# A sparse layer's index selection placed between projection units and attention pieces, and a reordered differential attention

## The reference

```python
def dsa_mixer(h, w_in, w_out, cos_a, sin_a, cos_i, sin_i):      # sparse layer A
    q, k, v, qi, ki, wi = split(h @ w_in)     # 16 heads of q, 4 of k and v, 8 index heads, 1 index key, 8 weights
    q, k, qi, ki = (partial_rope(t) for t in (q, k, qi, ki))
    wi = wi * IDX_WEIGHT_SCALE
    score = sum_h relu(qi_h @ ki.T) * wi_h                       # one score per query and key
    score = where(key in a visible chunk, score, -inf)
    sel = top_k(score, 64)                                       # 64 keys for every query
    o = softmax(q @ k[sel].T * 64 ** -0.5) @ v[sel]
    return o @ w_out

def diff_attention(h, w_qkv, w_o, ...):                          # layer C, 272 tokens
    q, k, v = split(h @ w_qkv)                                   # 8 heads, two maps c = 0, 1 of 64 columns each
    p = softmax(where(key <= query, q_c @ k_c.T * 64 ** -0.5, min))
    a = p[0] - lam * p[1]
    o = rmsnorm(a @ v, subln_g) * (1 - lambda_init)              # over the 128 columns of a head
    return o @ w_o
```

## Time and profile before

| what | before |
| --- | --- |
| median of 3 runs | 1735.62 us |
| lowest and highest | 1734.61 and 1742.96 us |
| the profiled execution, its own time | 1721.73 us |
| its span (first to last instruction) | 1719.9 us |
| granted TensorE clock, mean | 0.994 |
| PE, DVE, ACT busy | 96%, 61%, 44% of the span |

### The profile page before, as it was taken

How to read it: one execution, slowest core, us unless ns; L and a number is a source line. 1 busy time by engine, 2 the same in 40 slices (tenths; PEclk the granted TensorE clock), 3 DMA queues, 4 the chain that set the end, 5 groups by cost and what they waited for, 6 DMA issues and landing times.

```text
span 1719.9 us, 30972 instructions
## 1 busy us (share of the span) xinstructions
PE 1656.5 (96%) x12658; PEld 1548.7 (90%) x12658; DVE 1051.0 (61%) x1261; ACT 757.0 (44%) x1007; POOL 6.4 (0%) x21
## 2 busy tenths in 40 slices
PE   7899999998999999999999999999999999999998
PEld 5858999987899998999987999979999796789997
DVE  7785765458666556666457665466554647576653
ACT  3345553432655434444445444444443336454442
POOL 0000000010000000000000000000000000000000
PEclk9989999999999999999999999999999999999999
DMA  7602566633146675556722556635575351235671
GB/s 168 165 25 74 171 187 180 190 101 105 44 147 194 172 196 167 173 179 185 194 76 90 179 171 190 174 101 171 172 207 158 111 182 51 67 123 180 197 205 61
DMA packets 346674, 252.99 MB, mean 147 GB/s; under 512 B 32574, under 2 KB 345820, under 8 KB 346604
## 3 DMA queue, kind: packets, MB, share of 16 engines
q1 hardware_dynamic: 345136, 250.00, 49.4%
q10 hardware_dynamic: 1468, 2.02, 0.4%
HBM read 250.95 MB, written 1.05 MB: 147 GB/s over the span
## 4 chain that ended last, share of the span: by engine, by line
PE 82%; DVE 12%; ACT 4%; DMA 1%; issue 1%; ACTq 0%; DVEq 0%; SPq 0%
PE acc L457 25%; PE acc L458 25%; PE acc L459 25%; DVE w_low L1313 2%; PE acc L610 2%; PE spare L588 1%; DVE xg_low L1357 1%; ACT w_high L915 1%; PE acc L596 1%; DVE x_state L1508 1%; DVE squares L1342 1%; PE acc L473 1%; DVE evac_a L1506 1%; ACT xg_high L920 1%; PE acc L844 0%
## 5 line engine op out<-in xcount | busy, mean ns | idle before, releaser
L1313 DVE TENSOR_TENSOR w_low<-w_raw,w_high 128x2048 fp32r<-128x2048 f32 (+3 forms) x229 | 540.6, 2361 | 415.5 <-ACT w_high L915 415.4
L457 PE MATMUL acc<-xg_high,w_high 128*128 128x272 f32 (+4 forms) x2592 | 743.9, 287 | 14.7 <-DVE w_low L1313 7.6
L915 ACT ACTIVATE w_high<-w_raw 128x2048 fp32r<-128x2048 f32 (+3 forms) x229 | 451.4, 1971 | 684.4 <-PE acc L459 645.4
L458 PE MATMUL acc<-xg_low,w_high 128*128 128x272 f32 (+4 forms) x2592 | 737.8, 285 | 0.0
L459 PE MATMUL acc<-xg_high,w_low 128*128 128x272 f32 (+4 forms) x2592 | 735.7, 284 | 0.0
L457 PEld LDWEIGHTS acc<-xg_high,w_high 128*128 128x128 f32 (+3 forms) x2592 | 485.9, 187 | 32.0 <-issue 14.4
L458 PEld LDWEIGHTS acc<-xg_low,w_high 128*128 128x128 f32 (+3 forms) x2592 | 484.7, 187 | 3.7 <-issue 3.3
L459 PEld LDWEIGHTS acc<-xg_high,w_low 128*128 128x128 f32 (+3 forms) x2592 | 484.8, 187 | 0.2
L457 PE MATMUL acc<-hidden_high,w_high 128*128 128x256 f32 (+1 forms) x1216 | 345.2, 284 | 2.2 <-DVE w_low L1313 2.1
L459 PE MATMUL acc<-hidden_high,w_low 128*128 128x256 f32 (+1 forms) x1216 | 344.5, 283 | 0.0
L458 PE MATMUL acc<-hidden_low,w_high 128*128 128x256 f32 (+1 forms) x1216 | 344.4, 283 | 0.0
(11 more groups left out here) (198 smaller groups left out, 1062.9 us busy)
## 6 DMA issues: line engine op xcount, KB each, us to landing
w_raw<-in_ffn_w_dram SPq DMA_DIRECT2D x88, 1024.0 KB, 5.3
w_raw<-in_ffn_w_dram SPq DMA_DIRECT2D x32, 1408.0 KB, 7.0
w_raw<-in_mlp_w_up_dram SPq DMA_DIRECT2D x32, 1024.0 KB, 5.4
w_raw<-in_mlp_w_down_dram SPq DMA_DIRECT2D x32, 1024.0 KB, 5.6
w_raw<-in_attn_w_qkv_dram SPq DMA_DIRECT2D x12, 1024.0 KB, 5.1
w_raw<-in_a_w_in_dram SPq DMA_DIRECT2D x18, 256.0 KB, 4.4
w_raw<-in_a_w_in_dram SPq DMA_DIRECT2D x4, 1024.0 KB, 8.1
w_raw<-in_a_w_out_dram SPq DMA_DIRECT2D x4, 1024.0 KB, 5.0
```

What stands on the lines that cost most here:

```text
L457: pe.matmul(dst, high_w, high, start=first, stop=False)
L458: pe.matmul(dst, high_w, low, start=False, stop=False)
L915: act.activation(whi[c % 2][:, 0:SIZES[c]], raw[c % 2][:, 0:SIZES[c]], ACT.Copy).then_inc(S["w_high"], 1)
L1313: dve.tensor_tensor(wlo[c % 2][:, s], raw[c % 2][:, s], whi[c % 2][:, s].bitcast(F32), ALU.subtract)\
```

## The change

In the sparse layer the chunks are reordered (index queries, index key, values with the index weights, keys, four of queries). The key unit makes its 128 columns once. Values and weights come out by tokens, as `acc[token, column]`, so their transposes go; two more small matmuls give the norm by tokens. The rope works on unscaled units that ACT copies to `plain` (part of `mixer_out`); the norm is multiplied into `cos_a` and `sin_a`. The rope turns, the eight index products (all in one bank, `spare1`) and the selection rounds are written between the k-steps of the units, the units' evacuations, and the pieces of the attention. The attention takes all pieces of block 0 and then those of block 1; the selection of block 1 and the last query rope stand beside the pieces of block 0. The 17 fillers go.

In layer C the chunks come as values, keys, queries; the value transposes stand between units; the scores of pieces 0 and 1 stand ahead of unit 11. The query scale is folded into a second norm row (`rstd2`). PE adds the causal mask by a matmul of the identity with the mask constants into the same bank; the row maximum and the exponentials read PSUM directly. `difference` combines the maps once with a ratio of the row sums, and the division comes with ACT's copy of the output. DVE copies the transposed probabilities, not ACT. Pieces go by blocks; block 0 is normalized while block 1's pieces run. The second chunk of w_o is split beside piece 4. In the third feed-forward layer's up projection 28 fp32r matmuls take the place of 7 float32 fillers.

```diff
-        Gemm("a_in", [KD * 256] * 2 + [KD * 136] + [KD * 256] * 6, 9, dmas=[1, 1, 3, 4, 4, 4, 4, 1, 1]),
+        Gemm("a_in", [KD * 256] * 2 + [KD * P] + [KD * (KV_COLS + IDX_HEADS)] + [KD * 256] * 5, 9,
+             dmas=[1, 1, 2, 2, 1, 4, 4, 4, 4]),
...
+            def turn_raw(r, tiles):
+
+                pe.wait_ge(S["rope_raw"], r + 1)
+                if r == 7:
+                    bank = acc[1][:, 1]
+                else:
+                    bank = sp[0][:, r % 2]
+                    if r >= 2:
+                        pe.wait_ge(S["rope_read"], r - 1)
+                pe.matmul(bank[:, 0:tiles * SEQ], rotA, plain[r % 4][:, 0:tiles], start=True, stop=True)\
+                    .then_inc(S["rope_turned"], 1)
+
+            def index_logits(q):
+
                 i, m = q // 4, q % 4
-                if q == 1:
-                    pe.wait_ge(S["wi_ready"], 1)
-                if q >= 2:
-                    pe.wait_ge(S["idx_relu"], q - 1)
+                if q == 0:
+                    pe.wait_ge(S["rope_done"], 3)
+                else:
+                    pe.wait_ge(S["idx_relu"], q)
                 for c in range(2):
                     r = slice(c * HD, (c + 1) * HD)
-                    ins = pe.matmul(sp[q % 2][:, c, 0:(i + 1) * P], qiA[r, m, i * P:(i + 1) * P],
+                    ins = pe.matmul(sp[1][:, c, 0:(i + 1) * P], qiA[r, m, i * P:(i + 1) * P],
                                     kiA[r, 0:(i + 1) * P], start=True, stop=True)
                 ins.then_inc(S["idx_full"], 1)
...
+            def values_by_token(j):
+
+                c, u, wide_ = g.c0 + j, g.u0 + j, KV_COLS + IDX_HEADS
+                pe.wait_ge(S["w_low"], c + 1)
+                pe.wait_ge(S["rope_raw"], 2)
+                for i in range(2):
+                    t = slice(META + i * P, META + (i + 1) * P)
+                    for k in range(KD):
+                        if i == 0 and k == 4:
+                            turn_raw(2, 1)
+                        if i == 1 and k == 6:
+                            index_logits(0)
+                        hw, lw = cols(c, k * wide_, (k + 1) * wide_)
+                        dst = acc[u % 2][:, i, 0:wide_]
+                        pe.matmul(dst, XH[:, k, t], hw, start=k == 0, stop=False)
+                        pe.matmul(dst, XH[:, k, t], lw, start=False, stop=False)
+                        ins = pe.matmul(dst, XL[:, k, t], hw, start=False, stop=k == KD - 1)
+                ins.then_inc(S["w_used"], 1)
+
+            wide(g, 0, META, SEQ, xg_waits(PAIRS))
+            sum_squares(SEQ, 1, tokens=True)
+            wide(g, 1, META, SEQ, between={4: lambda: turn_raw(0, 2)})
+            wide(g, 2, META, SEQ, tiles=key_twice, M=1, between={6: lambda: turn_raw(1, 2)}, free=(S["rope_raw"], 1))
+            values_by_token(3)
+            wide(g, 4, META, SEQ, between={0: lambda: index_logits(1), 5: lambda: index_logits(2)},
+                 free=(S["rope_raw"], 3))
+            pe.wait_ge(S["v_ready"], n.add("v_ready"))
+            wide(g, 5, META, SEQ, between={1: lambda: index_logits(3), 3: lambda: turn_raw(3, 2),
+                                           6: lambda: index_logits(4)})
+            wide(g, 6, META, SEQ, between={2: lambda: index_logits(5), 4: lambda: turn_raw(4, 2),
+                                           6: lambda: index_logits(6)}, free=(S["rope_raw"], 4))
+            wide(g, 7, META, SEQ, between={2: lambda: index_logits(7), 4: lambda: turn_raw(5, 2)},
+                 free=(S["rope_raw"], 5))
+            wide(g, 8, META, SEQ, between={4: lambda: turn_raw(6, 2)}, free=(S["rope_raw"], 6))
+            pe.wait_ge(S["rope_raw"], 7)
+            keep_busy(acc[1][:, 0], 1)
+            turn_raw(7, 2)
...
-            keep_busy(acc[0][:, 0], 17)
-            attention([(i, m) for m in range(8) for i in range(2)],
+            pe.wait_ge(S["idx_relu"], 8)
+            pe.wait_ge(S["rope_done"], 7)
+            attention([(i, m) for i in range(2) for m in range(8)],
...
+            def make_scores(p):
+
+                i, h = pieces[p]
+                nk, d0 = (i + 1) * P + META, i * P + META
+                if p >= 2:
+                    pe.wait_ge(S["exp_done"], before + p - 1)
+                for c in range(2):
+                    r = slice(c * HD, (c + 1) * HD)
+                    pe.matmul(sp[p % 2][:, c, 0:nk], qC[r, h, i * P:(i + 1) * P], kC[r, h, 0:nk], start=True, stop=False)
+                for c in range(2):
+                    ins = pe.matmul(sp[p % 2][:, c, d0:nk], ident, cst[:, C_CAUSAL + META:C_CAUSAL + META + P],
+                                    start=False, stop=True)
+                ins.then_inc(S["s_full"], 1)
...
+            for j in range(1, 11):
                 wide(g, j, 0, T2)
-            turn_v(g, 8, [(0, P), (P, P), (2 * P, META)])
+                if 4 <= j < 10:
+                    turn_values(j - 4)
+            pe.wait_ge(S["v_ready"], n.add("v_ready", 6))
+            pe.wait_ge(S["dve_evac"], g.r0 + 9)
+            make_scores(0)
+            make_scores(1)
+            wide(g, 11, 0, T2)
             begin(G["w_o"])
-            keep_busy(acc[0][:, 0], 2)
-            attention([(i, h) for h in range(DIFF_HEADS) for i in range(2)],
-                      lambda i, h: [(qC[c * HD:(c + 1) * HD, h, i * P:(i + 1) * P],
-                                     kC[c * HD:(c + 1) * HD, h, 0:(i + 1) * P + META]) for c in range(2)],
-                      lambda i: [(0, k * P, P) for k in range(i + 1)] + [(0, (i + 1) * P, META)],
-                      lambda i, h, c, kt, nk: vC[0:nk, kt, h * P:(h + 1) * P],
-                      "probs_ready", [8, 4] + [1] * 14)
+            N = len(pieces)
+            for p in range(N + 2):
+                if 2 <= p + 1 < N and p:
+                    make_scores(p + 1)
+                if 1 <= p <= N:
+                    if 2 <= p <= DIFF_HEADS:
+                        keep_busy(acc[0][:, (p - 1) % 2], 1, P)
+                    turn_probs(p - 1)
+                if p >= 2:
+                    make_out(p - 2)
...
+            for j in range(3):
+                rope_copy(j, j, 1 if j == 2 else 2)
+                split(g.c0 + j + 2)
+            split(g.c0 + 5)
+            sem_, value = unit_full(g, 3)
+            act.wait_ge(sem_, value)
+            act.wait_ge(S["dve_evac"], g.r0 + 4)
+            for i in range(2):
+                ins = act.activation(vA[:, i, :], acc[(g.u0 + 3) % 2][:, i, 0:KV_COLS], ACT.Identity,
+                                     scale=tokrstd[:, i:i + 1])
+            ins.then_inc(S["v_ready"], 1)
+            index_relu(0)
+            index_relu(1)
+            for j in range(4, 9):
+                rope_copy(j - 1, j, 2)
+                split(g.c0 + j + 2)
+                for q in {4: (2, 3), 5: (4, 5), 6: (6, 7)}.get(j, ()):
+                    index_relu(q)
...
+            def exps(p):
+
+                act.wait_ge(S["s_read"], before + p + 1)
+                if p >= 2:
+                    act.wait_ge(S["pt_full"], before + p - 1)
+                nk = (pieces[p][0] + 1) * P + META
+                for c in range(2):
+                    ins = act.activation(Pr[p % 2][:, c, 0:nk], sp[p % 2][:, c, 0:nk], ACT.Exp,
+                                         bias=rowneg[:, p % 4, c:c + 1], accum_out=rowsum[:, p % 4, c:c + 1])
+                ins.then_inc(S["exp_done"], 1)
...
+            def rope_raw(r, tiles, dst):
+
+                dve.wait_ge(S["rope_turned"], r + 1)
+                if r >= 2:
+                    dve.wait_ge(S["rope_done"], r - 1)
+                x, y = tb[r % 2][:, 0:tiles, 0:SEQ], sq[r % 2][:, 0:tiles, 0:SEQ]
+                bank = acc[1][:, 1] if r == 7 else sp[0][:, r % 2]
+                dve.tensor_tensor(x, plain[r % 4][:, 0:tiles], across(cosA[:], tiles), ALU.mult)\
+                    .then_inc(S["dve_evac"], 1)
+                dve.tensor_tensor(y, bank[:, 0:tiles * SEQ].rearrange("p (k t) -> p k t", k=tiles),
+                                  across(sinA[:], tiles), ALU.mult).then_inc(S["rope_read"], 1)
+                dve.wait_ge(S["rope_read"], r + 1)
+                dve.wait_ge(S["dve_evac"], g.r0 + r + (1 if r < 3 else 2))
+                dve.tensor_tensor(dst, x, y, ALU.add).then_inc(S["rope_done"], 1)
...
+            split(g.c0 + 2)
+            rope_raw(0, 2, qiA[:, 0:2])
+            split(g.c0 + 3)
+            rope_raw(1, 2, qiA[:, 2:4])
+            split(g.c0 + 4)
+            rope_raw(2, 1, kiA[:].unsqueeze(1))
+            unit_wait(g, 3)
+            for i in range(2):
+                ins = dve.tensor_scalar(wiA[:, i, :], acc[(g.u0 + 3) % 2][:, i, KV_COLS:KV_COLS + IDX_HEADS],
+                                        tokrstd[:, i:i + 1], IDX_SCALE, ALU.mult, ALU.mult)
+            ins.then_inc(S["dve_evac"], 1)
+            dve.wait_ge(S["dve_evac"], g.r0 + 4)
+            split(g.c0 + 5)
+            index_score(0)
+            split(g.c0 + 6)
+            index_score(1)
```

(81 more changed lines are left out.)

308 lines of the change are left out of this document (180 added, 128 removed).

## The result

The changed kernel takes **1742.05 us**, the median of 20 runs (1733.37 to 1749.29), against 1733.24 for the kernel before on the same chip (20 runs, 1715.85 to 1742.96). The ratio is 1.0061, with a 95% interval of 1.0035 to 1.0088. So it is 0.6% slower. I had forecast 1728.3, with a range of 1718.5 to 1737: the sign and the range were wrong. The profiled execution took 1744.29 us, its span 1742.5, where that of before had 1721.73 and 1719.9.

A forecast was written before the change was run, and what follows sets the result against it. TensorE, busy 96% of the span, was the bound, leaving its idle time and filler to win. 3.4 + 5.4 - 2.1 + 0.85 - 0.2 = 7.35 us less than the median 1735.62 gave 1728.3, range 1718.5 to 1737.

The forecast's parts named there:

- The ReLU waits: Sparse projections: TensorE waits for ScalarE's ReLUs before index products, 3.2, 2.2, 1.75 and 1.75 us, 8.9 together.
- Rival (b): Sparse projections: ScalarE reaches the ReLUs before TensorE needs them, so no waits; gain 16.3 us, total 1719.3; chance 0.20.
- Projections and selection up to the score pass: Sparse layer: VectorE's first score pass starts at 99.9 us, 11.7 sooner than 111.57.
- The pieces: Sparse attention: block 0 16.4 us, split 2.3, block 1 15.5, tail 6.5; the projection starts at 140.6.
- The failed step: Sparse attention: TensorE's clock taken to stay full, with block 1's pieces at 2.06 us each.
- (d): Sparse attention: clock falls in block 0's pieces, not back before the projection; 15.5 us more, total 1743.8; chance 0.07.
- (a): Sparse attention: clock falls after 95 us and comes back; gain 4.5 us, total 1731; chance 0.18.
- The base: Whole kernel: the profiled execution's 0.8% shortfall from the median, 1721.73 against 1735.62, carried over to the forecast.
- Last attention: Last attention: start gains 5.4 us, pieces lose 2.1 (waits 1.8 and 1.2), end gains 0.85.
- Untouched stages: Stages the change does not rewrite: no term in the sum, except 0.2 us lost to fillers before the third ffn.

The follow-up runs named there:

- order: The changed kernel with ScalarE's ReLUs of the index scores each one place earlier, ahead of the weight splits; 1731.32 us.
- tuned: The changed kernel with earlier index ReLUs, short fillers in the sparse pieces and six of 512 columns in the last attention; 1716.98 us, 0.9933 of the kernel before.
- c_fill: The changed kernel with 15 fillers of 512 columns ahead of transposes in the last attention; 1739.89 us over 4 runs.
- c_only: The kernel before with only the change's last attention and the 28 wide fillers, its sparse layer kept; 1739.53 us, ratio 1.0058.
- fill_start: The changed kernel with fillers among the sparse projections and ahead of the first two pieces' transposes, none later; 1746.03 us in one execution.
- the 68 runs: Those of 98 runs of the unaltered kernel before, taken beside the experiments, with a mean clock of 0.989 or less; median 1737.0 us.
- the 30: Those of 98 runs of the unaltered kernel before, taken beside the experiments, with a mean clock of 0.99 or more; median 1718.7 us.
- fill: The changed kernel with fillers where TensorE would wait among the sparse projections, behind them and in the attention's pieces; 1730.07 us, 1.0011 of the kernel before.
- after_places: The changed kernel with its five new small tiles placed behind all others, restoring the old addresses; 1738.34 us, 1.0039 of the kernel before.
- fill_pieces: The changed kernel with fillers only ahead of the transposes of sparse pieces 3 to 9; 1742.36 us in one execution.
- s_tuned: The sparse layer with earlier index ReLUs and short fillers, with the last attention of the kernel before; 1717.81 us, 0.9905 of the kernel before.

## Why the prediction was wrong, step by step

- **The ReLU waits** (3.2, 2.2, 1.75, 1.75): right, 8.3 for 8.9. Rival (b) is out in the changed kernel. Its price for the waits was 8.9; `order` starts the score pass 12.2 us earlier, 8.0 of it waits and an estimated 2.7 the half clock behind the longest (25 matmuls at 0.213 us in place of 0.118, and a product of 0.80 for 0.49).
- **Projections and selection up to the score pass**: 105.0 for 99.9. All of it arises before DVE has split the output projection's first chunk (97.05 for 91.8); from there it is 8.0 us for 8.1. An estimated 2.7 of the 5 us are the half clock behind the ReLU wait at 49 to 52 us, the rest is not traced. I had priced that wait (3.2), but not the clock behind it.
- **The pieces**, 16.4 + 2.3 + 15.5 + 6.5 = 40.7 from score pass to projection: right in sum where block 1 has full clock (`tuned` 40.8, `c_fill` 40.9), 49.5 in the changed kernel. The sum is right in part by luck: block 0 took 17.7, the rest behind the split 20.8 for 22.0. And 16.4 is not what its terms add up to: eight pieces of 0.79 + 0.39 and the six rounds that the code has there, with 0.3 and 1.95, make 17.6.
- **The failed step** is the argument on the clock, which left block 1's seven and a half pieces at 2.06 us each and gave (d) 0.07. Against (d) I wrote that "block 1's fill PE", against (a) that "PE never idles 5 us at a stretch". The runs showed that the clock falls behind a wait of 2.7 us, or of 0.6 and less in stretches of pieces (`c_only`, `fill_start`), and that pieces that fill PE may leave it there: 20 us of them (120 to 140) did not end it. It cost 8.7 us in the changed kernel's profile (49.5 against the 40.9 of the same pieces in `c_fill`) and 12.4 where it lasted to the end. The rows held a warning: PE idle or lightly loaded ran at 0.50, and the fillers that the change removes stood ahead of the pieces and among those of the last attention; but the old order loses the clock with its 17 fillers too.
- **Near (d) by luck**: its 1743.8 lies close to the 1742.05, but its 15.5 us were for block 1 alone. Against the 1714.4 of my sum the profiled execution took 29.9 more: about 14.1 in the first layer (5.1 ahead of the score pass, the rest in the pieces), 8.6 in the block of the last attention, 7.4 in the rest. The 13.9 that I added for the base hid half of it.
- **The base**: I moved the profiled 1721.7 to the median 1735.6 as if the 0.8% were even over the kernel. They are two kinds of run, 18 us apart, and the profile was of the rarer kind; what a change does to each kind had to be asked apart. Against the 68 runs (1737.0) the changed kernel is 5 us slower, and the stages add up to it: its first layer is 7.2 shorter than the old one without the clock (158.8 against 166.0 in `c_only`), the last attention 4.7 and the untouched stages some 7 longer (an estimate: 166.0 is the one profile that shows the old layer without the clock). Against the 30 (1718.7) it is 23 slower.
- **Last attention**: start (1.9 us after unit 11) right, mask pair 0.64 for 0.57, the gap 2.1 for 1.8, the second 1.6 for 1.2. At full clock the block gains 1.6 (said 3.95). What was missing is that each gap is followed by 6 to 8 us at 0.50. How long varies with the same code: the block takes 166.7 us in `fill` and `order`, 169.8 in the changed kernel, 172.9 in `after_places` and 174.5 in `fill_pieces` (some 1.5 of it a dip near the block's start, as in `s_tuned`). The row maximum from PSUM takes 0.72 us in the chain of the changed kernel, 720 ns from SBUF before: priced at nothing, rightly.
- **Untouched stages**: priced at nothing; they took 7 us. With the old addresses the two MLP stages are 6.3 us shorter in the profile, the whole 3.7.

## What to carry to other kernels

Before filler is removed or a wait is added on TensorE, price the stretch behind it at both clock levels, and ask what in it would bring the clock back: a stretch of short matmuls that looks fully busy may not, and may in another execution of the same code. One profile shows one of these; look at the spread and the mean clock of the runs before taking one profile as the base. A filler longer than the wait it fills gives back what the clock wins (`c_fill`), and a shorter one may not keep the clock every time (`tuned`). A new small tile belongs behind the large ones, where it moves nothing that matmuls stream; that is measured here for one tile and four addresses.
